# Small TensorE products in another order: array tiles alternate, first summands of all sums ahead of the second ones

## The chip, the cores and the metric

The kernel runs on one core of one Trainium2 chip. The metric is the device time of one execution in microseconds, the median of several runs. One core has TensorE (matrix products; in the profile PE for the matmuls and PEld for the weight loads), VectorE (DVE), ScalarE (ACT), GpSimd (POOL) and SyncE (SP, which here only issues DMAs).

## The reference

One layer of a decoder: a head group with an RWKV-7 recurrence and a head group with a gated linear recurrence side by side, then a mixture of experts, for a prompt of 1024 tokens and 8 decode tokens. The change touches the RWKV-7 recurrence alone. Per head (8 heads of 64 channels) the reference computes, token by token:

```python
def _wkv7_scan(r, decay, k, v, a_vec, b_vec, s0):
    def step(s, inp):
        r_t, w_t, k_t, v_t, a_t, b_t = inp
        sa = jnp.einsum('bhij,bhj->bhi', s, a_t)
        s = s * w_t[:, :, None, :] + sa[..., None] * b_t[:, :, None, :] + v_t[..., None] * k_t[:, :, None, :]
        return s, jnp.einsum('bhij,bhj->bhi', s, r_t)
```

Around it stand the input projection, small low-rank gates, a normalisation per head, the output projection (`w_out`) and the experts.

## The kernel before, in words

All data are f32. The kernel does not go token by token. It takes the heads in pairs (`j`, 4 pairs: 2 x 64 channels fill 128 partitions) and the tokens in chunks of 64, solves the dependence inside a chunk by products with a triangular inverse, and carries the state from chunk to chunk.

For each pair `j` TensorE first projects the tokens (`project_tile`, L791), and then makes two **passes** (`hf` = 0, 1), one for each half of the 1024 tokens. A pass has two groups (`g` = 0, 1) of 256 tokens. Each group has its own buffers (`grp[g]`) and its own four of the eight banks of PSUM (`q.bank(0)` to `q.bank(3)`). In all there are 4 pairs x 2 passes x 2 groups = 16 groups. Inside a group `hh` is one of the two heads of the pair (partitions 0 to 63 or 64 to 127, the slice `r`), `a` one of two blocks of 128 tokens (two chunks each), and `c` the first or second chunk of a block (partitions 0 to 63 or 64 to 127 where tokens are on partitions).

The order of TensorE in a pass is written out by hand:

- grams (L944) and transposes (L968), whose results VectorE masks and ScalarE copies;
- stages akv, u, w, z, each for group 0 and then for group 1, through the helper `stage` (L929); these products use all 128 rows and columns of the array, and between two stages VectorE or ScalarE brings the result to SBUF;
- stage `rt_mm` for group 0, then for group 1, in three parts: part 1 (L929), 4 products into `bank(0)` with 128 rows and 64 columns of the array, the columns chosen by the head; part 2 (L929), 8 products of 64 rows and 64 columns into `bank(2 + c)`; part 3 (L1004, L1005), 8 sums of two products each, 64 rows and 64 columns, into other columns of `bank(2 + c)`. The rows of parts 2 and 3 go by `c`, the columns by `hh`, so that `(c, hh)` is one of four quadrants of the array. The last product increments `rt_mm`;
- `y_products(0)`: 4 sums of two products (L1010, L1012), 128 rows, the columns by the head;
- `state_step(0, 0)`: the new state (L1030, two products) and its share of y (L1034, two products);
- `y_products(1)`, `state_step(0, 1)` to `(0, 3)`, `state_step(1, 0)` to `(1, 3)`, with grams or chunks of the next pair's projection (`keys_chunk`) between them, and then the normalisation of y.

On VectorE `transitions(g)` waits for `rt_mm`, adds into `rh` (L1830), makes four transition matrices `tt` (L1833) and copies part 3's sums into `into` (L1835). `next_state(g, n)` (L1841) waits for the state step's product and adds `into`. VectorE's order is transitions(0), next_state(0, 0), transitions(1), next_state(0, 1) and so on. `state_step(g, 0)` waits for `tt` and `rh`, every other state step for the sum before it.

The order of `heads()` before was `for hh in range(2): for a in range(2)`. It sets the order in grams, akv, u, w, z, the three parts of `rt_mm`, and y.

Behind the fourth pair come the output projection (L1104), the routing, and 20 steps of the experts. SP issues the loads of the projection weights by counts of TensorE's products (`win_mm`), the first loads of the experts' weights after the output projection (`wo_mm`), and later ones by TensorE's counts in the experts.

Of the kernel before, what the change touches and what calls it, by code (L numbers as in the profile page):

```python
# [21 lines left out]
HEAD = 64  # L22
# [40 lines left out]
def build(nc, x_all, c_t, shift_t, wkv0, conv0, lru0, state_conv, w_ada, b_ada, w_in, w_lo, prm, mu_lo,  # L63
# [9 lines left out]
    with ExitStack() as ctx:  # L73
# [356 lines left out]
        V, A, T, G = nc.vector, nc.scalar, nc.tensor, nc.gpsimd  # L430
# [313 lines left out]
        def _(pe):  # L744
# [72 lines left out]
            for c in range(3):  # L817
                c0, w = COLS[c]
                pe.wait_ge(win_out, c + 1)
                for m in range(2):  # L820
                    for g in range(4):
                        k = 2 * g + m
                        mm = T.matmul(ps[32 * g:32 * g + 32, c, 0:w], wlo[:, k, 128:160], hT[:, k, c0:c0 + w],
                                      start=(m == 0), stop=(m == 1))
# [3 lines left out]
            for c in range(3):  # L828
# [3 lines left out]
                         stop=True).then_inc(ad_mm, 1)  # L832
            pe.wait_ge(ld_const, 16 * 9)
            pe.wait_ge(ld_samp, 16 * 4)
            for j in range(NJ):
# [8 lines left out]
                def one_head(t):  # L844
                    return t.rearrange("p (h c) -> p h c", c=HEAD)[:, :, 0]
# [68 lines left out]
                for hf in range(2):  # L914
# [2 lines left out]
                    AR0, AR1, bb, k2, Bh, Kh, eP, rkp = kept[hf]  # L917
                    AR = ARs[hf]
                    def heads():
                        for hh in range(2):  # L920
                            for a in range(2):
                                yield hh, a, slice(HEAD * hh, HEAD * hh + HEAD)

                    def stage(g, name, waits, products, last=True):
                        gi = 2 * it + g
                        for w in waits:
                            pe.wait_ge(HV[w], gi + 1)
                        for out, lhs, rhs in products:
                            mm = T.matmul(out, lhs, rhs, start=True, stop=True)  # L929
                        if last:  # L930
                            mm.then_inc(HV[name], 1)
# [8 lines left out]
                    def grams(m, n, g, src):  # L940

                        q = grp[g]
                        for hh, a, r in heads():
                            mm = T.matmul(q.bank(2 * n + hh)[:, 256 * a:256 * a + 256], src[r, toks(g, a)],  # L944
                                          ARs[m][r, :, toks(g, a)], start=True, stop=True)
                        mm.then_inc(HV[("gram_b", "gram_k")[n]], 1)
# [27 lines left out]
                    for g in range(2):  # L974
                        q = grp[g]
                        stage(g, "akv_mm", ("tok_out",),
                              [(q.bank(3)[:, P * a + HEAD * hh:P * a + HEAD * hh + HEAD], q.ak[:, hh, a, 0, :],
                                q.vtok[:, a, HEAD * hh:HEAD * hh + HEAD]) for hh, a, r in heads()])
                    pe.wait_ge(p_in, 80 * (j + 1))
                    for g in range(2):  # L980
                        q = grp[g]
                        stage(g, "u_mm", ("dt_out", "akv_out"),
                              [(zunit(g, 0)[:, :, a, hh], pinv(hf, g)[:, hh, a], q.z[:, :, a, hh]) for hh, a, r in heads()])
                    for g in range(2):
                        q = grp[g]
                        stage(g, "w_mm", ("u_out",),
                              [(zunit(g, 1)[:, :, a, hh], q.dtg[:, hh, a, 0, :], q.u[:, :, a, hh]) for hh, a, r in heads()])
                    for g in range(2):
                        q = grp[g]
# [3 lines left out]
                    for g in range(2):  # L993
                        q = grp[g]
                        stage(g, "rt_mm", ("z_out",),
                              [(q.bank(0)[r, P * a:P * a + P], q.z[:, 0, a, hh, :], q.dtg[:, hh, a, 1, :])
                               for hh, a, r in heads()] +
                              [(q.bank(2 + c)[r, HEAD * a:HEAD * a + HEAD], q.zt[HEAD * c:HEAD * c + HEAD, 0, a, r],
                                q.btok[HEAD * c:HEAD * c + HEAD, a, r]) for c in range(2) for hh, a, r in heads()], False)
                        for c in range(2):  # L1000
                            t_ = slice(HEAD * c, HEAD * c + HEAD)
                            for hh, a, r in heads():
                                out = q.bank(2 + c)[r, 128 + HEAD * a:128 + HEAD * a + HEAD]
                                T.matmul(out, q.btok[t_, a, r], q.zt[t_, 1, a, r], start=True, stop=False)  # L1004
                                mm = T.matmul(out, q.ktok[t_, a, r], q.vtok[t_, a, r], start=False, stop=True)  # L1005
                        mm.then_inc(HV["rt_mm"], 1)
                    def y_products(g):
                        q = grp[g]
                        for hh, a, r in heads():
                            T.matmul(q.bank(1)[r, P * a:P * a + P], q.z[:, 1, a, hh, :], q.dtg[:, hh, a, 1, :],  # L1010
                                     start=(a == 0), stop=False, skip_group_check=True)
                            T.matmul(q.bank(1)[r, P * a:P * a + P], q.vtok[:, a, r], q.ak[:, hh, a, 1, :],  # L1012
                                     start=False, stop=False, skip_group_check=True)

                    def state_step(g, n):
# [20 lines left out]
                        if n == 3:  # L1036
                            mm.then_inc(HV["y_mm"], 1)

                    y_products(0)
                    state_step(0, 0)  # L1040
                    y_products(1)
                    for n in range(1, 4):
                        state_step(0, n)
# [21 lines left out]
                    for n in range(4):  # L1065
                        mm = T.matmul(bank[5][:, 2 * n:2 * n + 2], tmp[:, P * n:P * n + P], one_head(blk_mean),
                                      start=True, stop=True)
# [6 lines left out]
                    for n in range(4):  # L1074
                        for hh in range(2):
                            mm = T.matmul(bank[7][HEAD * hh:HEAD * hh + HEAD, P * n:P * n + P],
                                          gnorm[:, 2 * n + hh:2 * n + hh + 1].to_broadcast([P, HEAD]), ident,
                                          start=True, stop=True)
# [5 lines left out]
            for b_, lhs, rhs in ((4, w_up, pwd), (5, a_up, pad_), (6, g_up, pgd)):  # L1084
                for j in range(NJ):
                    mm = T.matmul(bank[b_][:, DEC * j:DEC * j + DEC], lhs[:, P * j:P * j + P],
                                  rhs[:, PAD + SEQ:PAD + NTOK], start=True, stop=True)
# [3 lines left out]
                     stop=True).then_inc(SAMP["s_norm"][0], 1)  # L1091
            for a, w_ in ((0, rg), (1, ig)):
                for j in range(NJ):
                    mm = T.matmul(bank[7][:, SN * a + DEC * j:SN * a + DEC * j + DEC], w_[:, j, :], s_xc[:, j, :],
                                  start=True, stop=True)
# [47 lines left out]
            def route_h2(i):  # L1143
# [3 lines left out]
                for k in range(KC):  # L1147
# [8 lines left out]
                     stop=True).then_inc(SAMP["s_bonmm"][0], 1)  # L1156
            pe.wait_ge(*SAMP["s_vec"])
            pe.wait_ge(*SAMP["s_lexp"])
            for q in range(6):
                mm = T.transpose(bank[6 + q // 4][0:SN, P * (q % 4):P * (q % 4) + P], s_vflat[:, SN * q:SN * q + SN], ident)  # L1160
# [20 lines left out]
            for i in (7, 8):  # L1181
# [7 lines left out]
                     stop=True).then_inc(rank_mm, 1)  # L1189
            pe.wait_ge(tile_col, 1)  # L1190
            T.matmul(bank[3][0:1, 0:NTILE], tcol[0:NTILE], ident[0:NTILE, 0:NTILE], start=True,
                     stop=True).then_inc(tile_row, 1)
            for n in range(18):
                if n % 6 == 0:
                    pe.wait_ge(hot_ready, n // 6 + 1)
                c = n % NCT
                mm = T.matmul(bank[2][COLT * c:COLT * c + COLT, 0:P], wt[:, n // 9, n % 9, :], uu[:, n, :],
                              start=(n < NCT), stop=(n >= 18 - NCT))
# [61 lines left out]
            for i, t in enumerate(LAST):  # L1260
# [5 lines left out]
                for n in range(2):  # L1266
                    for a in range(2):
                        mm = T.matmul(ps[0:rt, 2 * (i % 4) + n, :], wdiag[t][0:rt, P * a:P * a + rt],  # L1268
                                      yg[t][0:rt, a, 512 * n:512 * n + 512], start=(a == 0), stop=(a == 1))
# [1005 lines left out]
```

## Time and profile before

| | before |
|---|---|
| median of 3 runs | 1248.86 us (1244.17 to 1253.95) |
| the profiled execution | 1248.42 us, its span 1246.4 us |
| TensorE matmuls busy | 1089.4 us, 87% |
| VectorE busy | 639.0 us, 51% |
| ScalarE busy | 306.0 us, 25% |
| granted TensorE clock, mean | 0.933 |

The span is the time from the first to the last instruction of the program on the core. Busy times of different engines overlap. The granted clock is the share of TensorE's full clock that the chip gave it: 1.00 is 2.4 GHz, 0.5 is 1.2 GHz. Starts of matmuls are recorded, their ends are modelled; one product of f32 leaves two matmul records and two weight loads.

### The profile page before, as it was taken

The page shows a single profiled execution, that of the slowest core. Times are in us where ns is not written, and L with a number is a line of the kernel's source. Part 1 is how long each engine was busy: PE and PEld are TensorE (multiplying, and loading weights), DVE is VectorE, ACT ScalarE, POOL GpSimd, SP SyncE. Part 2 cuts the span into 40 slices and gives each one's busy share as a digit, 9 for nine tenths or more (in the row PEclk, how much of TensorE's full clock was granted, in tenths as well). Part 3 has the DMA queues.
Part 4 walks back from the last instruction along what each step waited for, and adds up shares of the span by engine and source line. Part 5 has one row for each costly group of instructions (what it writes and reads, how often), then busy time and mean ns, then how long its engine had stood idle before and what let it go on. Part 6 is the DMA issues. An engine that isn't in the chain of part 4 may idle for free.

```text
span 1246.4 us, 18940 instructions
## 1 busy us (share of the span) xinstructions
PE 1089.4 (87%) x7309; PEld 635.8 (51%) x7309; DVE 639.0 (51%) x1298; ACT 306.0 (25%) x576; POOL 87.6 (7%) x142
## 2 busy tenths in 40 slices
PE   5899997999979999899997799997388989899692
PEld 3445566766667666676666654554232333233131
DVE  7326684268942689425894349988501111111158
ACT  2324241142411424114141240111011111111246
POOL 4210100000000010000100010000000000000050
PEclk9999999999989999889999889998588999899976
DMA  9965310011100111000140061224867795866472
GB/s 354 295 218 187 103 34 2 1 34 52 35 1 1 34 52 34 1 1 23 30 154 1 1 236 51 74 90 148 324 219 286 257 351 198 294 219 211 147 288 118
DMA packets 56625, 160.78 MB, mean 129 GB/s; under 512 B 23512, under 2 KB 23720, under 8 KB 50776
## 3 DMA queue, kind: packets, MB, share of 16 engines
q1 hardware_dynamic: 46376, 126.40, 29.8%
q0 software_dynamic: 6560, 22.07, 5.1%
q10 hardware_dynamic: 3600, 11.11, 2.3%
q8 instruction: 57, 0.93, 0.3%
q14 instruction: 32, 0.26, 0.1%
HBM read 341.48 MB, written 22.59 MB: 292 GB/s over the span
## 4 chain that ended last, share of the span: by engine, by line
PE 54%; DVE 23%; SPq 8%; DMA 8%; issue 5%; ACT 1%; POOL 0%; DVEq 0%; POOLq 0%; ACTq 0%
PE ps L791 14%; PE ps L1104 7%; PE ps L1214 5%; PE ps L929 5%; PE ps L1229 4%; DVE arena L1753 3%; DVE arena L1755 3%; DMA arena<-in_w_ada 3%; SPq L534 3%; DMA arena<-in_w_dn 3%; PE ps L1030 2%; SPq L565 1%; SPq L561 1%; DVE arena L1768 1%; PE ps L751 1%
## 5 line engine op out<-in xcount | busy, mean ns | idle before, releaser
L791 PE MATMUL ps<-arena 128*128 128x348 f32 (+1 forms) x1008 | 306.7, 460 | 2.5 <-DVE arena L1620 2.5
L791 PEld LDWEIGHTS ps<-arena 128*128 128x128 f32 x1008 | 189.4, 191 | 114.6 <-issue 19.3
L1214 PE MATMUL ps<-arena 128*32 128x512 f32 x1280 | 149.2, 615 | 9.7 <-DMA arena<-in_w_gu 8.4
L2150 DVE COPY arena<-ps 128x1024 f32<-128x1024 f32 x20 | 24.5, 1226 | 177.1 <-PE ps L1229 177.1
L1104 PE MATMUL ps<-arena 128*128 128x512 f32 x256 | 114.1, 601 | 0.0
L1214 PEld LDWEIGHTS ps<-arena 128*32 128x32 f32 x1280 | 43.6, 113 | 110.8 <-issue 101.4
L1229 PE MATMUL ps<-arena 128*32 128x512 f32 x640 | 78.9, 637 | 12.6 <-DMA arena<-in_w_dn 12.2
L929 PE MATMUL ps<-arena 128*128 128x128 f32 (+3 forms) x896 | 86.2, 278 | 3.8 <-DVE arena L1825 2.8
L929 PEld LDWEIGHTS ps<-arena 128*128 128x128 f32 (+2 forms) x896 | 79.4, 179 | 10.6 <-DVE arena L1825 3.6
L1104 PEld LDWEIGHTS ps<-arena 128*128 128x128 f32 x256 | 48.3, 193 | 56.8 <-issue 56.7
L1319 ACT ACTIVATE arena<-ps 128x348 f32<-128x348 f32 (+1 forms) x54 | 24.8, 460 | 205.4 <-PE ps L791 198.5
L1229 PEld LDWEIGHTS ps<-arena 128*32 128x32 f32 x640 | 21.1, 115 | 55.7 <-issue 55.0
L1268 PE MATMUL ps<-arena 128*128 128x512 f32 (+1 forms) x72 | 37.5, 687 | 8.7 <-DMA arena<-slot_scr,arena 8.7
L944 PE MATMUL ps<-arena 64*128 64x256 f32 x256 | 35.5, 411 | 9.5 <-DVE arena L1875 6.7
L1753 DVE TENSOR_TENSOR arena<-arena 64x30 f32<-64x30 f32 (+14 forms) x120 | 39.8, 332 | 6.6 <-POOL arena L688 2.6
L2144 DVE TENSOR_TENSOR arena<-arena,ps 128x256 f32<-128x256 f32 x20 | 8.5, 423 | 67.0 <-ACT arena L1503 67.0
L1841 DVE TENSOR_TENSOR arena<-ps,arena 128x64 f32<-128x64 f32 x64 | 14.3, 224 | 54.8 <-PE ps L1030 54.8
L1755 DVE TENSOR_TENSOR arena<-arena 64x30 f32<-64x30 f32 (+14 forms) x120 | 38.8, 323 | 4.1
L1503 ACT ACTIVATE arena<-ps 128x256 f32<-128x256 f32 x20 | 7.7, 385 | 133.7 <-PE ps L1214 133.7
L725 POOL DMA_INDIRECT arena<-h_scr,arena x20 | 18.9, 945 | 274.9 <-PE ps L1206 210.2
L682 POOL MEMSET arena<- 128x2048 f32 x4 | 7.2, 1806 | 440.1 <-DVE arena L1717 440.1
L1402 ACT ACTIVATE arena<-ps 128x512 f32<-128x512 f32 (+1 forms) x48 | 25.3, 526 | 43.0 <-PE ps L929 42.8
(421 smaller groups left out, 1515.0 us busy)
## 6 DMA issues: line engine op xcount, KB each, us to landing
arena<-in_w_gu SPq DMA_DIRECT2D x336, 512.0 KB
arena<-in_w_dn SPq DMA_DIRECT2D x84, 1024.0 KB
arena<-in_w_ada SPq DMA_DIRECT2D x24, 1024.0 KB, 6.1
arena<-in_w_in SPq DMA_DIRECT2D x20, 512.0 KB, 3.8
slot_scr<-arena ACTq DMA_DIRECT2D x20, 512.0 KB, 4.1
arena<-in_x_all SPq DMA_DIRECT2D x16, 512.0 KB, 4.9
arena<-in_w_out SPq DMA_DIRECT2D x8, 512.0 KB, 7.4
h_scr<-arena SPq DMA_DIRECT2D x8, 512.0 KB, 2.6
```

The costliest lines, as they stand in the source:

```text
L534: sp.dma_start(exgu_f[c][:, cols], src, cond=ch[c]).then_inc(ld_gu[h], 16)
L791: mm = T.matmul(ps[0:rows, c, 0:w], lhs(k), hT[:, k, c0:c0 + w], start=(k == 0), stop=(k == KC - 1))
L929: mm = T.matmul(out, lhs, rhs, start=True, stop=True)
L944: mm = T.matmul(q.bank(2 * n + hh)[:, 256 * a:256 * a + 256], src[r, toks(g, a)], ARs[m][r, :, toks(g, a)], start=True, stop=True)
L1030: mm = T.matmul(out[r], q.tt[r, n, :], S[r, n % 2, :], start=True, stop=True)
L1104: mm = T.matmul(ps[0:rt, 2 * (i % 2) + n, :], yT[:, k, r0:r0 + rt], wout[:, k, 512 * n:512 * n + 512], start=(k == 0), stop=(k == KC - 1))
L1214: mm = T.matmul(ps[r_, 2 + b, :], xgt[b][:, k, r_], exgu[c][:, k, :], start=(k == 0), stop=(k == KC - 1))
L1229: mm = T.matmul(ps[r_, 6 + n, :], hidt[b][:, q, r_], exdn[c][:, q, 512 * n:512 * n + 512], start=(q == 0), stop=(q == 1))
L1268: mm = T.matmul(ps[0:rt, 2 * (i % 4) + n, :], wdiag[t][0:rt, P * a:P * a + rt], yg[t][0:rt, a, 512 * n:512 * n + 512], start=(a == 0), sto ...
L1402: A.activation(dst, src, ACT.Copy).then_inc(HV[name], 1)
L1753: link(TT(prod, m[:, 0:k, k:k + 1].to_broadcast([64, k, w]), m[:, k:k + 1, k + 1:32].to_broadcast([64, k, w]), ALU.mult))
L1755: last = TT(m[:, 0:k, k + 1:32], m[:, 0:k, k + 1:32], prod, ALU.add)
```

## The change

The two loops of `heads()` change places, part 2 has the chunk inside, part 3 goes through all four quadrants with the first summand of a block's sums and then with the second, and the y products do all first summands before the second ones. The products, their operands, outputs and waits are the same.

```diff
                     def heads():
-                        for hh in range(2):
-                            for a in range(2):
+                        for a in range(2):
+                            for hh in range(2):
                                 yield hh, a, slice(HEAD * hh, HEAD * hh + HEAD)
...
-                                q.btok[HEAD * c:HEAD * c + HEAD, a, r]) for c in range(2) for hh, a, r in heads()], False)
-                        for c in range(2):
-                            t_ = slice(HEAD * c, HEAD * c + HEAD)
-                            for hh, a, r in heads():
-                                out = q.bank(2 + c)[r, 128 + HEAD * a:128 + HEAD * a + HEAD]
-                                T.matmul(out, q.btok[t_, a, r], q.zt[t_, 1, a, r], start=True, stop=False)
-                                mm = T.matmul(out, q.ktok[t_, a, r], q.vtok[t_, a, r], start=False, stop=True)
+                                q.btok[HEAD * c:HEAD * c + HEAD, a, r]) for hh, a, r in heads() for c in range(2)], False)
+                        for a in range(2):
+                            for last, left, right in ((False, q.btok, q.zt[:, 1]), (True, q.ktok, q.vtok)):
+                                for hh in range(2):
+                                    r = slice(HEAD * hh, HEAD * hh + HEAD)
+                                    for c in range(2):
+                                        t_ = slice(HEAD * c, HEAD * c + HEAD)
+                                        mm = T.matmul(q.bank(2 + c)[r, 128 + HEAD * a:128 + HEAD * a + HEAD],
+                                                      left[t_, a, r], right[t_, a, r], start=not last, stop=last,
+                                                      skip_group_check=True)
                         mm.then_inc(HV["rt_mm"], 1)
                     def y_products(g):
                         q = grp[g]
                         for hh, a, r in heads():
                             T.matmul(q.bank(1)[r, P * a:P * a + P], q.z[:, 1, a, hh, :], q.dtg[:, hh, a, 1, :],
                                      start=(a == 0), stop=False, skip_group_check=True)
+                        for hh, a, r in heads():
                             T.matmul(q.bank(1)[r, P * a:P * a + P], q.vtok[:, a, r], q.ak[:, hh, a, 1, :],
                                      start=False, stop=False, skip_group_check=True)
```

## Rows read from the trace of the kernel before

**Rows 1.** The page: TensorE's busy time (share) and records; the chain by engine.
```profile
PE 1089.4 (87%) x7309; PEld 635.8 (51%) x7309; DVE 639.0 (51%) x1298; ACT 306.0 (25%) x576; POOL 87.6 (7%) x142
...
PE 54%; DVE 23%; SPq 8%; DMA 8%; issue 5%; ACT 1%; POOL 0%; DVEq 0%; POOLq 0%; ACTq 0%
```
**Rows 2.** Table of stretches, TensorE alone: rt of group 1, y of group 0.
```profile
core 0: us, PE busy (x), PEclk, DMA share, GB/s
...
344.86:347.16 2.30, 2.30 (x58) 1.00 0.00 0
347.16:348.67 1.51, 1.51 (x18) 1.00 0.05 11
```
**Rows 3.** Timeline (start, us, engine, line, count), TensorE: rt of group 1, y.
```profile
344.86 0.42 PEld L929 LDWEIGHTS ps<-arena 128*64 128x64 f32 x8
...
345.46 0.34 PEld L929 LDWEIGHTS ps<-arena 64*64 64x64 f32 x16 [0.17 <-issue]
...
345.74 0.28 PE L1004 MATMUL ps<-arena 64*64 64x64 f32 x2
...
345.86 0.28 PE L1005 MATMUL ps<-arena 64*64 64x64 f32 x2
...
345.97 0.33 PE L1004 MATMUL ps<-arena 64*64 64x64 f32 x4
...
346.84 0.28 PE L1004 MATMUL ps<-arena 64*64 64x64 f32 x2
...
347.16 0.43 PE L1010 MATMUL ps<-arena 128*64 128x128 f32 x2
...
347.43 0.38 PE L1012 MATMUL ps<-arena 128*64 128x128 f32 x2
...
347.65 0.44 PE L1010 MATMUL ps<-arena 128*64 128x128 f32 x4
...
348.14 0.38 PE L1010 MATMUL ps<-arena 128*64 128x128 f32 x2
...
348.67 0.33 PE L1030 MATMUL ps<-arena 64*64 64x64 f32 x4
```
**Rows 4.** The same timeline: VectorE's work, and the third state step on TensorE.
```profile
344.97 0.42 DVE L1830 TENSOR_TENSOR arena<-arena,ps 128x256 f32<-128x256 f32 x1 [3.84 <-PE ps L1005]
345.31 0.85 DVE L1833 SCALAR_TENSOR_TENSOR arena<-arena,ps 128x64 f32<-128x64 f32 x4
...
349.12 0.23 DVE L1841 TENSOR_TENSOR arena<-ps,arena 128x64 f32<-128x64 f32 x1 [2.63 <-PE ps L1030]
...
350.36 0.41 DVE L1835 COPY arena<-ps 128x256 f32<-128x256 f32 x1
...
351.01 0.22 DVE L1841 TENSOR_TENSOR arena<-ps,arena 128x64 f32<-128x64 f32 x1 [0.24 <-PE ps L1030]
...
351.29 0.33 PE L1030 MATMUL ps<-arena 64*64 64x64 f32 x4 [0.28 <-DVE arena L1841]
```
**Rows 5.** Timelines: products that alternate tiles, and the grams.
```profile
351.45 0.28 PE L1034 MATMUL ps<-arena 64*64 64x64 f32 x4
...
272.22 1.97 PE L872 MATMUL ps<-arena 128*64 128x128 f32 x32
...
326.69 3.80 PE L944 MATMUL ps<-arena 64*128 64x256 f32 x32 [0.69 <-ACT arena L1324]
```
**Rows 6.** Stretches from rt to rt, pairs 1 to 3: us, five engines, clock, DMA.
```profile
342.57:382.33 39.76, 33.09 (x350) 27.14 (x349) 14.47 (x35) 7.12 (x16) 0.00 (x0) 0.87 0.00 1
498.68:539.64 40.96, 34.85 (x350) 29.09 (x349) 14.47 (x35) 7.12 (x16) 0.00 (x0) 0.83 0.00 1
655.98:693.42 37.44, 30.66 (x349) 24.78 (x348) 14.47 (x35) 7.01 (x16) 0.00 (x0) 0.95 0.01 1
```
**Rows 7.** Groups by line and shape, all passes: records, busy us, mean ns.
```profile
L1004 PE MATMUL ps<-arena 64*64 64x64 f32 x256 | 22.0, 227 | 0.0
...
L1010 PE MATMUL ps<-arena 128*64 128x128 f32 x128 | 20.1, 285 | 0.0
```

## The prediction

> **What bounds the kernel now.** I read the page first: TensorE is busy 87% of the span and carries 54% of the chain that ended last, VectorE 23% [rows 1]. So an order on TensorE is worth something only in a stretch where that chain runs through TensorE without a break. The next view is a table of stretches inside one pass (group 1 of the first pass of pair 1): the stage `rt_mm` (2.30 us) and the y products (1.51 us) are filled by TensorE completely, at a granted clock of 1.00, the 2.4 GHz level [rows 2]. What is saved there moves everything behind it, until some other engine is late.
>
> The timeline of the same stretch tells how the array is used [rows 3]. A product leaves two matmul records: L1004 has 256 records for 16 groups of 8 products [rows 7]. The stage has three parts. Part 1, four products into the two column halves of bank 0, runs from 344.86 to 345.46, 0.60 us. Part 2, eight products in the four quadrants, from 345.46 to 345.74, 0.28 us: its 16 weight loads all lie within 0.34 us, so the four quadrants run side by side already, although the program gives each quadrant two products in a row. Part 3, sixteen products (L1004, L1005), from 345.74 to 347.16, 1.42 us. Here each quadrant gets four products in a row, and the rows show a staircase: x2, x2 alone, then three steps of x4, x4, then x2, x2 alone. Eight pairs of products take five steps, where two quadrants at most run together. The y products show it with halves: x2, x2, then x4, x4, then x2, x2: three steps of 0.49, 0.49 and 0.53 us.
>
> My reading of both: matmuls start in program order, and a tile of the array takes four records ahead. Four in a row for one tile leave the next tile free to start at once (parts 1 and 2); eight in a row hold it up until the fifth has started (part 3 and y).
>
> **The change part by part.** No instruction is added or removed, no DMA and no wait; every increment stays on the last product of its group. Only TensorE's order moves.
>
> (a) `heads()` now has the pair outside and the head inside. In akv, u, w and z every product fills all 128 rows and columns, so there is no other tile: nothing. In the grams a row half gets two products in a row, four records, within the reach above: 32 records of 256 columns stand in 3.80 us [rows 5], 0.11 us each, as long as a 128-column record alone in its half takes (0.109 us, below), so the halves overlap already: nothing. Parts 1 and 2: also nothing. A first start some 0.01 us sooner is the most I can see there, and I take 0.
>
> (b) Part 3, quadrants inside, summands outside. One quadrant alone does a pair (four records) in 345.97 - 345.74 = 0.23 us, 0.058 us a record. In the new order each quadrant still has eight records, but all four run together: 8 x 0.058 = 0.46 us. Behind the last record the next stage takes 0.09 us (the last lone pair starts at 346.84 and L1010 at 347.16, 0.32 less the 0.23 of its own records), and the four quadrants start one after another, three times about 0.014 us (16 loads of part 2, the last starting about 0.21 us after the first). Together 0.60 us instead of 1.42: **0.82 us a group**. Part 2 gives the same: 0.28 us for four rounds, 0.23 for four more, 0.09 behind.
>
> (c) The y products, first summands ahead. In one half a record takes 0.109 us (347.43 to 347.65 for two) and entering the form costs 0.05 (0.49 for the first four). Eight records in each half, side by side: 0.05 + 8 x 0.109 + about 0.11 behind and between = 1.03 us instead of 1.51: **0.48 us a group**. Part 1 again agrees: 0.60 us with four records in each half, plus 4 x 0.109.
>
> That alternating products overlap at all is shown in the trace: L872 alternates the column halves at every product, and 32 records of 128 columns stand in 1.97 us [rows 5], 0.06 us each against 0.109 alone. L1030 alternates quadrants at every product, and its four records are through in 0.16 us, 351.29 to 351.45 [rows 4, 5], where one quadrant after the other would need 0.23.
> The Trainium skill, page "TensorE: Matmul & The Clock Gate", Part 3 (The mechanism), speaks against (c): a weight load overlaps running matmuls only where the row group differs, and the column halves of y share all rows. L872 above disagrees with it. By that rule (c) would give nothing and (b) only the two row halves; what this makes of the sum is among the rivals.
>
> (d) What of it reaches the end. On TensorE the order in a pass is rt of group 0, rt of group 1, y of group 0, the first state step, y of group 1, the second state step. The first state step comes 0.82 + 0.82 + 0.48 = 2.12 us sooner. Its other wait, VectorE's transitions of group 0 (344.97 to about 346.2 [rows 4]), starts 0.82 sooner as well and is still done before. Then VectorE is late next: behind the first state sum (349.12) it does the transitions of group 1, whose last copy ends at 350.36 + 0.41 = 350.77, and the second sum starts at 351.01 after an idle of 0.24 us [rows 4]. All of this moves by 2.12; the 0.48 of group 1's y can only eat that idle time, less some 0.04 us for the hand-over: 0.20. From there a state step waits for VectorE's sum and the sum for the state step (L1030 at 351.29 idled 0.28 for it), so the rest of the pass keeps its length. **2.12 + 0.20 = 2.32 us a pass.** There are four pairs with two passes each, 16 groups [rows 7]: 8 x 2.32 = 18.6 us.
>
> Behind a pass nothing is tied to the clock on the wall: the next pair's projections wait for TensorE and ScalarE, the queue on SP loads the next weights by TensorE's counts, and the experts' first loads wait for the output projection (`wo_mm`). So the gain should stay. The profiled execution took 1248.42 us (0.44 under the median of 1248.86): 1248.42 - 18.6 = **1230 us**. With no VectorE limit it would be 8 x 2.60 = 20.8, 1228 us.
>
> **The clock as spread.** Between the `rt` stages of the two passes of a pair the granted clock falls to half for a while, and that stretch takes 40.96 us at a mean of 0.83 and 37.44 us at 0.95 [rows 6]; pair 1 takes 39.76 at 0.87, and pair 0 the same within 0.02 us. Which stretches are slow will be dealt anew when all moves by 2 us. Four like the best would be 149.8 instead of 157.9 us (-8), four like the worst 163.8 (+6). I take about 4 us either way.
>
> **The rivals.**
> 1. *Issue is the limit.* Parts 2 and 3 are 24 products in 1.70 us, 0.071 us each; if the sequencer gives no more, part 3 keeps its length but for a head start during part 1 (0.60 us for four products, 0.32 us to spare). Gain per rt 0 to 0.31, per pass 0.68 to 1.3, in all 5 to 10 us: 1238 to 1243. Against it: part 2 starts its loads at 0.014 us each, and the y staircase has the same shape at 0.12 us a product, where issue can't be the limit.
> The same page of the Trainium skill ("Wait — 56ns, not 53.3ns?") gives about 62 ns a matmul where the sequencer's microcode decodes; an estimate by it is 1234 us, and no run here shows which decoder is on.
> 2. *Column halves don't overlap.* Then y gives nothing and part 3 runs two-fold: 16 x 0.058 + 0.13 = 1.06, 0.36 a group, 0.72 a pass, 5.8 us: 1243. L872 and part 1 speak against it.
> 3. *The clock gives it back.* TensorE's work in a pass becomes shorter while its waits stay. From 37.44 to 39.74 us the mean falls from 0.95 to 0.87, about 6.8 us more at half clock for 2.3 us. To eat 18.6 us, each pair needs 14 us more of half clock: 1240 to 1249. The stretch in rows 2 ran at 1.00 throughout and gets denser, so I see no reason.
> 4. *Slower: tiles take turns.* If neighbours in other tiles ran one after the other, part 3 would need 16 x 0.117 + 0.13 = 2.0 us (+0.58) and y 8 x 0.219 + 0.16 = 1.91 (+0.40): 1.96 a pass, 16 us, 1264. It decides once fewer than about 1.4 tiles run together. L1030 and L872 speak against it.
>
> **How the numbers follow.** The forecast 0.66 (1222 to 1236: the sum, its bounds and the clock), rival 1 0.14, rival 2 0.04, rival 3 0.08, rival 4 0.03, and 0.05 for a clock even better than 1222. The range reaches from 1222 to 1240: the forecast and most of rival 1. One per cent, about what a measurement of this kernel can tell from no change, is 1236.4 on the faster side: faster 0.72 (the forecast, the 0.05 and a little of rival 1), no change 0.25 (the rest of rivals 1 to 3), slower 0.03.
>
> **What would show it.** Right: in the timeline, part 3 without staircase and about 0.6 us from its first record to the next stage, y about 1.03; rt stage about 1.48 us a group; VectorE's second sum with no idle before it; the stretch from the first `rt` record of group 0 to the third state step shorter by 2.3 us in all eight passes. Wrong: part 3 at 0.07 us a product (rival 1), y at 1.5 us (rival 2), a lower clock in `rt` (rival 3). The prediction fails most easily if something behind the passes that I take for tied to TensorE keeps its own time.

## The result

| | before | after |
|---|---|---|
| median | 1249.8 us (10 runs) | 1236.55 us (10 runs) |
| ratio to before, 95% interval | | 0.9914, 0.9887 to 0.9941 |
| the profiled execution, its span | 1248.42, 1246.4 us | 1234.13, 1232.2 us |
| TensorE matmuls busy | 1089.4 us | 1069.7 us |
| mean granted clock of the profiled execution | 0.933 | 0.927 |

The kernel became faster by about one per cent. The ratio gives a gain of 7 to 14 us, the two medians 13 us; 18.6 us were forecast. In two later comparisons, on two chips, the ratio was 0.9874 (0.9831 to 0.9918, e5_after) and 0.9899 (0.9865 to 0.9933, e12_after). The time lies in the stated range of 1222 to 1240 us, but above the 1222 to 1236 us that belonged to the forecast itself; the last 4 us of the range were there for rival 1.

In the code after the change the lines lie a little lower: part 3 is L1006, the y products L1013 and L1016, the state step L1034 and L1038, the state sum L1845. The timeline of the same stretch as [rows 3, 4], the first pass of pair 1 in the profile of after:

```profile
338.73 0.42 PEld L929 LDWEIGHTS ps<-arena 128*64 128x64 f32 x8
...
339.32 0.32 PEld L929 LDWEIGHTS ps<-arena 64*64 64x64 f32 x16 [0.17 <-issue]
...
339.60 0.65 PE L1006 MATMUL ps<-arena 64*64 64x64 f32 x32
...
340.18 0.66 PE L1013 MATMUL ps<-arena 128*64 128x128 f32 x8
...
341.20 0.33 PE L1034 MATMUL ps<-arena 64*64 64x64 f32 x4
...
341.65 0.22 DVE L1845 TENSOR_TENSOR arena<-ps,arena 128x64 f32<-128x64 f32 x1 [1.25 <-PE ps L1034]
...
342.89 0.42 DVE L1839 COPY arena<-ps 128x256 f32<-128x256 f32 x1
343.34 0.23 DVE L1845 TENSOR_TENSOR arena<-ps,arena 128x64 f32<-128x64 f32 x1
343.62 0.33 PE L1034 MATMUL ps<-arena 64*64 64x64 f32 x4 [0.57 <-DVE arena L1845]
```

The staircase is gone. Part 3 runs from 339.60 to 340.18, 0.58 us instead of 1.42, and y from 340.18 to 341.20, 1.02 us instead of 1.51. The second state sum (343.34) has no idle before it any more, and TensorE's wait for it grew from 0.28 us [rows 4] to 0.57. From the first `rt` record (337.29) to the third state step (343.62) are 6.33 us; before, 342.57 to 351.29, 8.72. That is 2.39 us, where 2.32 were forecast.

The table of stretches is the best ruler for the whole kernel, since one stretch is free of the clock: from the `rt` stage of a pair's second pass to that of the next pair's first pass. The columns are start:end, us, TensorE busy, granted clock, DMA share, GB/s. First before:

```profile
226.23:342.57 116.34, 112.41 (x690) 1.00 0.12 33
382.33:498.68 116.35, 112.40 (x689) 1.00 0.12 33
539.64:655.98 116.34, 112.40 (x690) 1.00 0.18 56
```

and after (here with all five engines):

```profile
223.32:337.29 113.97, 109.66 (x690) 75.07 (x689) 78.24 (x174) 36.42 (x64) 3.88 (x4) 1.00 0.13 33
374.61:488.60 113.99, 109.66 (x689) 75.07 (x688) 78.26 (x174) 36.42 (x64) 3.88 (x4) 1.00 0.12 33
527.17:641.12 113.95, 109.65 (x689) 75.07 (x688) 78.19 (x174) 36.41 (x64) 4.99 (x6) 1.00 0.18 57
```

Three times 2.36 to 2.39 us less, at a clock of 1.00 on both sides; 8 x 2.37 = 19.0 us. The stretches between the two passes of a pair, which answer to [rows 6], do not all show it:

```profile
337.29:374.61 37.32, 30.38 (x349) 24.71 (x349) 14.49 (x35) 7.12 (x16) 0.00 (x0) 0.86 0.00 1
...
641.12:678.44 37.32, 30.39 (x349) 24.71 (x348) 14.49 (x35) 7.12 (x16) 0.00 (x0) 0.86 0.01 1
```

For pair 1 it is 2.44 us (39.76 before), for pair 3 only 0.12 (37.44 before, at a clock of 0.95). And the last stretch, from the last pass's `rt` to the first product of the output projection, became longer, first before, then after:

```profile
693.42:724.36 30.94, 24.37 (x280) 0.77 0.24 84
```
```profile
678.44:709.79 31.35, 24.55 (x279) 0.65 0.23 82
```

So the profile itself points to the clock: 0.65 instead of 0.77 in a stretch whose work is 2.4 us shorter. Each run comes with its span and mean clock. As the clock has two levels, 1.00 and 0.5, the time at the half one is 2 x (1 - clock) x span; all times at half clock below are worked out in this way or, for single falls, read from the clock records of a trace. The experiments below ask two things: which edit saves the work, and whether it is the clock that takes part of it back.

### The profile page after: what moved, and what is told of

The parts are those of the page before. It is cut to its first block, busy times and chain, and to the rows that moved or that the text cites. A ratio compares the mean times of both kernels' runs of the same rounds, so it can differ in the third digit from the quotient of the medians.

```text
span 1232.2 us, 18940 instructions
## 1 busy us (share of the span) xinstructions
PE 1069.7 (87%) x7309; PEld 616.7 (50%) x7309; DVE 639.2 (52%) x1298; ACT 306.2 (25%) x576; POOL 87.6 (7%) x142
## 4 chain that ended last, share of the span: by engine, by line
PE 53%; DVE 25%; DMA 9%; SPq 7%; issue 5%; ACT 1%; POOL 0%; DVEq 0%; POOLq 0%; ACTq 0%
PE ps L791 14%; PE ps L1108 7%; PE ps L1218 6%; PE ps L929 5%; PE ps L1233 4%; DMA arena<-in_w_dn 3%; DVE arena L1757 3%; DVE arena L1759 3%; DMA arena<-in_w_ada 3%; SPq L534 2%; PE ps L1034 1%; DVE arena L1772 1%; SPq L561 1%; SPq L565 1%; PE ps L751 1%
## 5 line engine op out<-in xcount | busy, mean ns | idle before, releaser
L929 PEld LDWEIGHTS ps<-arena 128*128 128x128 f32 (+2 forms) x896 | 82.1, 184 | 10.1 <-DVE arena L1829 3.6
L1845 DVE TENSOR_TENSOR arena<-ps,arena 128x64 f32<-128x64 f32 x64 | 14.3, 224 | 42.4 <-PE ps L1034 42.1
```

## The experiments

All of them ran beside the kernel before. "Next-pair stretch" is the one of 116.34 us above, read in each profile.

**e1_part3: part 3 alone.** Against the kernel before:

```diff
-                        for c in range(2):
-                            t_ = slice(HEAD * c, HEAD * c + HEAD)
...
-                                T.matmul(out, q.btok[t_, a, r], q.zt[t_, 1, a, r], start=True, stop=False)
-                                mm = T.matmul(out, q.ktok[t_, a, r], q.vtok[t_, a, r], start=False, stop=True)
+                        for a in range(2):
+                            for last, left, right in ((False, q.btok, q.zt[:, 1]), (True, q.ktok, q.vtok)):
+                                for hh in range(2):
...
+                                    for c in range(2):
...
+                                                      left[t_, a, r], right[t_, a, r], start=not last, stop=last,
```

> Part 3 of the rt stage in the new order, all else as before. If a tile takes four records ahead (theory 1): part 3 without staircase, the rt stage 1.45 us a group instead of 2.30, y unchanged at 1.51. The first state step then comes 2 x 0.85 = 1.70 us sooner and nothing else does: the stretch from the second pass of a pair to the next pair, 116.34 us before, takes 114.64, and all eight passes give 13.6 us less what the clock takes. If the accumulating neighbours were what held part 3 up, the same; if the new order of heads() were needed for it (rival), part 3 stays above 1 us.

Measured: `rt` 1.47 us a group, and y 1.51 with its staircase. The next-pair stretch:

```profile
226.26:340.97 114.71, 110.77 (x690) 1.00 0.13 33
```

1.63 us less than before; 1.70 were expected. The median of 4 runs is 1234.05 us, ratio 0.9887 (0.9841 to 0.9933), with as much half clock as the kernel before beside it (165 us a run in both). Part 3 alone carries most of the work saved, and it needs no new `heads()`. Its ratio is that of the whole change (0.9874 to 0.9914): what the other half, the new y order, saves besides can't be seen in the time.

**e2_y: the y products alone.**

```diff
-                        for hh, a, r in heads():
+                        order = [(hh, a, slice(HEAD * hh, HEAD * hh + HEAD)) for a in range(2) for hh in range(2)]
+                        for hh, a, r in order:
                             T.matmul(q.bank(1)[r, P * a:P * a + P], q.z[:, 1, a, hh, :], q.dtg[:, hh, a, 1, :],
                                      start=(a == 0), stop=False, skip_group_check=True)
+                        for hh, a, r in order:
                             T.matmul(q.bank(1)[r, P * a:P * a + P], q.vtok[:, a, r], q.ak[:, hh, a, 1, :],
```

> The y products in the new order, all else as before. Theory 1: y takes 1.02 us instead of 1.51; the first state step comes 0.49 us sooner, and of the second 0.49 VectorE's transitions let 0.20 through: the stretch to the next pair 116.34 - 0.69 = 115.65 us, 5.5 us in all. If VectorE did not limit (rival): 116.34 - 0.98 = 115.36.

```profile
230.67:346.33 115.66, 111.43 (x689) 1.00 0.12 33
186.85:230.67 43.82, 38.19 (x349) 0.73 0.01 1
```

The next-pair stretch falls by 0.68 us, as expected to 0.01: of the second y only what VectorE's idle time allows. But the time did not fall: 1250.29 us median of 10, ratio 1.0023 (0.9997 to 1.0049). Mean clock 0.926 instead of 0.934; 185 us at half clock instead of 165. The second row shows one place: between the first two passes the clock was 0.73 on average, and the stretch took 43.82 us instead of 39.74. The four stretches of this kind hold 58 us of half clock in e2's profile and 38 in that of before.

**e3_heads: `heads()` and part 2 alone,** part 3 and y in the old order.

> Only heads() and part 2 of rt in the new order; part 3 and y in the old one. Theory 1: at most two products per tile in a row before, so nothing changes: part 1 and 2 at 0.60 and 0.28 us, the stretch to the next pair 116.34 us, within 0.05. Rival (alternating at every product is worth something for the grams and parts 1 and 2): the stretch is shorter by 0.1 us or more.

```profile
228.12:344.46 116.34, 112.33 (x689) 1.00 0.12 33
```

116.34 us, nothing, and 1248.01 us, ratio 1.0001 (0.9972 to 1.0029). In the grams and in parts 1 and 2, two products per tile in a row were no hindrance.

**e4_adjacent and e6_adjacent: as after, but both summands of a sum side by side again,** so that each tile gets two products in a row:

```diff
-                            for last, left, right in ((False, q.btok, q.zt[:, 1]), (True, q.ktok, q.vtok)):
-                                for hh in range(2):
...
-                                    for c in range(2):
...
+                            for hh in range(2):
...
+                                for c in range(2):
...
+                                    T.matmul(out, q.btok[t_, a, r], q.zt[t_, 1, a, r], start=True, stop=False,
...
+                                    mm = T.matmul(out, q.ktok[t_, a, r], q.vtok[t_, a, r], start=False, stop=True,
...
-                        for hh, a, r in heads():
                             T.matmul(q.bank(1)[r, P * a:P * a + P], q.vtok[:, a, r], q.ak[:, hh, a, 1, :],
```

> As after, but the two summands of a sum stand side by side again, in part 3 and in y: each tile gets two products (four records) in a row, and then the next tile. Theory 1 (four records are taken ahead): as fast as after, rt 1.45 and y 1.02 us, the stretch to the next pair 113.97 us; first summands ahead of second ones is worth nothing by itself. Rival (a second summand right behind the first waits for it, and that held the others up): the staircase comes back in part, rt above 1.7 us, y above 1.2, the stretch above 114.7 us.

```profile
225.74:339.96 114.22, 109.96 (x689) 1.00 0.12 33
```

114.22 us: neither 113.97 nor above 114.7. Per group `rt` takes 1.55 us and y 1.07, so two products per tile in a row cost about 0.1 and 0.05 us here; the staircase does not come back. "First summands ahead" is thus worth 0.25 of the 2.37 us a pass, the alternation of tiles the rest. Whether the 0.25 us comes from a second summand right behind its first, as the rival has it, or from two products in a row whatever they are, e4 does not tell; part 2, which has no sums, took 0.28 us in either order. e4's 1231.94 us (4 runs) with a clock of 0.931 led to the idea that the alternation at every y product lowers the clock. e6 tested this beside e5_after (the changed kernel again) on one chip.

> The changed kernel, unchanged, beside the next three and the kernel before. Over the runs so far the kernel before spends 165 us of a run at the half clock (mean clock 0.934), the changed one 184 us (0.925), e2_y 185 us, e1_part3, e3_heads and e4_adjacent 165 to 169; a microsecond at half clock costs 0.31 to 0.35 us. Theory 2: the new y order brings more half clock, about 20 us a run, which costs 6 to 7 us of the 18.9 us of work saved: clock 0.925 again and 1236 us. Rival: the lower clock belongs to the chip or the hour of the first runs: clock 0.933 and 1230 us.

> e4_adjacent once more, now beside the changed kernel on one chip. Theory 2 (the alternation of halves at every y product lowers the clock, pairs of products do not): clock 0.931, 1232 us, some 4 us under e5_after. Rival (e4's four runs were lucky, both have the same short y): clock and time as e5_after within 1.5 us, or slower by the 0.25 us a pass that the work is longer (2 us).

e5_after: 1233.42 us, ratio 0.9874 (0.9831 to 0.9918), mean clock 0.929, between what was expected (0.925, 1236 us) and its rival (0.933, 1230 us). e6_adjacent: 1234.73 us, 0.9876 (0.9827 to 0.9925), 0.930. The two are the same within these intervals, and theory 2 falls in this form: the alternation at every y product is not what moves the clock.

**e8_three: six records per quadrant in a row.** Part 3 of after with three products of each quadrant, then the fourth of each:

```diff
+                        for n0, n1 in ((0, 3), (3, 4)):
+                            for hh in range(2):
...
+                                for c in range(2):
...
+                                    for n in range(n0, n1):
+                                        a, last = n // 2, n % 2 == 1
+                                        left, right = (q.ktok, q.vtok) if last else (q.btok, q.zt[:, 1])
...
```

> The changed kernel, but part 3 gives each quadrant three products (six records) in a row and then the fourth. If a tile takes four records ahead: the next quadrant starts when the third record of the one before starts, 0.117 us later, three times: part 3 is longer by 0.35 us a group (rt 1.80), 0.70 a pass, and the stretch to the next pair takes 113.97 + 0.70 = 114.67 us. If more are taken ahead (rival): 113.97; if fewer, above 115.

The rule holds, and its price was higher. In the records a quadrant's first three start at 339.720, 339.779 and 339.837, and the next quadrant's first at 339.843, 6 ns behind the third of six. The fourth quadrant starts 0.46 us behind the first (340.184), since from the second on a quadrant's first record needs about 0.107 us (339.843 to 339.949) and not 0.058; the last round pays it again. The next-pair stretch:

```profile
223.93:338.85 114.92, 110.64 (x689) 1.00 0.12 33
```

0.95 us over after, where 0.70 was expected. Its time, of a single run, is 1242.93 us.

**e7_fill: TensorE's waits filled.** The changed kernel with 38 products that compute nothing needed, and a wait for `dt_out` ahead of some of them:

```diff
+                    def filler(n):
+                        for _ in range(n):
+                            T.matmul(bank[0][:, 0:384], ident, rg[:, 0:3, :], start=True, stop=True, skip_group_check=True)
...
                         pe.wait_ge(HV["y_roots"], 2 * it)
                         grams(1, 0, 1, bb)
+                        filler(3)
                         pe.wait_ge(HV["half_done"], it)
                     grams(hf, 1, 1, k2)
+                    if hf:
+                        filler(3)
                     for g in range(hf, 2):
                         turn(hf, g)
...
+                    if hf == 0:
+                        pe.wait_ge(HV["dt_out"], 2 * it + 3)
+                    if hf == 0 or j == NJ - 1:
+                        filler(2)
                     pe.wait_ge(HV["y_roots"], 2 * it + 1)
...
+            for _ in range(4):
+                T.matmul(bank[0][:, 0:384], ident, rg[:, 0:3, :], start=True, stop=True, skip_group_check=True)
             pe.wait_ge(HV["half_done"], 2 * NJ)
```

> The changed kernel with products that compute nothing needed, put where TensorE waits: in the first pass of each pair 2 (before the row of squares), 3 (before the mask of y is done) and 3 (before the last turn), in the last pass 2 and 4. Each is 384 columns, about 0.67 us at full clock, into a bank that is free. If idle TensorE in these places is what lowers the clock (theory 2): the stretch between the two passes of a pair loses its half clock (37.3 us before filling, 34 to 35 with a clock above 0.97), the clock rises to 0.945 or more and the time falls by 8 to 12 us under e5_after. Rival (the clock falls for another reason, or the fillers stand in the way): the stretch stays at 37 us or grows by up to 5 us.

1220.51 us, ratio 0.9773 (0.9730 to 0.9816), mean clock 0.946. Where the clock stayed up, the stretch between the two passes takes 34.49 us:

```profile
338.02:372.51 34.49, 31.67 (x366) 1.00 0.00 1
```

against 37.32 at 0.86 in after. This holds for two of the four pairs; in the other two the clock fell to half 8.4 us behind `rt`, for 10.2 and 6.8 us, and the stretch took 38.03 and 36.52 us. More work on TensorE made the kernel 13 us faster than e5_after beside it. The timeline of after shows the waits that were filled:

```profile
353.60 1.05 PE L1070 MATMUL ps<-arena 128*128 128x2 f32 x8 [1.44 <-ACT arena L1430]
...
359.57 1.54 PE L944 MATMUL ps<-arena 64*128 64x256 f32 x8 [1.90 <-DVE arena L1879]
362.43 1.97 PE L968 MATMUL ps<-arena 128*128 128x128 f32 x8 [1.32 <-DVE arena L1780]
```

Behind the second of these waits eight gram records take 1.54 instead of 1.13 us, and behind the third the transposes 1.97 instead of 1.07: these are products at half clock.

**e9_before_fill, e10_fill, e12_after: the change with the clock out of the way.** The filler of e7 in the kernel before, in the changed one again, and the changed kernel without it, on one chip.

> The kernel before, with the same products in TensorE's waits as e7_fill (they compute nothing needed). Theory 3: the change saves 18.6 us of work whatever the clock does, and the clock takes a part back because more of a run is at half clock (175 to 184 us against 165). With the waits filled in both kernels the clock has little to take: this kernel about 1237 us (before less some 12 us), e10_fill 18 to 19 us under it. Rival (the change saves less work than the stretches say, or something behind the passes keeps its own time): the two filled kernels differ by 13 us or less, as the unfilled ones do.

> The changed kernel with the filled waits once more, beside e9_before_fill, on one chip. 1220 us and a clock of 0.946 as in e7_fill, 18 to 19 us under e9_before_fill by theory 3, 13 or less by its rival.

> The changed kernel on the chip of the three above. Theory 3: more half clock than the kernel before beside it (0.925 to 0.929 against 0.933), 1234 to 1237 us, and at equal half clock, taken at 0.33 us a microsecond, 18 to 19 us less than before.

| | median us | ratio to before | mean clock | us at half clock |
|---|---|---|---|---|
| before (11 runs) | 1252.24 | 1 | 0.931 | 173 |
| e12_after (6) | 1237.97 | 0.9899 (0.9865 to 0.9933) | 0.924 | 188 |
| e9_before_fill (6) | 1234.5 | 0.9863 (0.9834 to 0.9892) | 0.954 | 113 |
| e10_fill (6) | 1219.05 | 0.9732 (0.9700 to 0.9764) | 0.949 | 124 |

The change is worth 14.3 us without fillers here and 15.5 us with them: neither 18 to 19 nor 13. Half clock is not equal in the filled kernels either, 124 against 113 us. The profiles say where. First e9, then e10: between the passes, to the next pair, and the last stretch.

```profile
186.63:223.54 36.91, 34.35 (x365) 1.00 0.01 2
223.54:339.88 116.34, 112.41 (x690) 1.00 0.12 33
683.30:711.09 27.79, 25.29 (x292) 0.94 0.18 65
```
```profile
188.81:223.29 34.48, 31.66 (x365) 1.00 0.01 2
223.29:338.93 115.64, 111.35 (x689) 0.99 0.12 33
671.97:698.24 26.27, 23.64 (x292) 0.89 0.18 60
```

Between the passes both have the full clock, and the change shows its 2.43 us. In the next stretch, and in one more like it, e10 has lost all but 0.70 of 2.37: the clock fell to half 8.6 us behind the `rt` stage, in the run of state steps, for 3.4 us.

**e11_chain: one product more in the state steps.**

```diff
                     for n in range(1, 4):
                         state_step(0, n)
+                        if n == 1:
+                            T.matmul(bank[2][:, 0:256], ident, rg[:, 0:2, :], start=True, stop=True, skip_group_check=True)
```

> e10_fill with one more product of 256 columns that computes nothing needed, between the second and the third state step of each pass, where TensorE now waits 0.57 us for VectorE. In the profiles of the changed kernel the clock fell 9.4 us behind the last pass's rt stage, in the run of state steps, for 27 us; in those of the kernel before 16.9 us behind it, for 17. If the longer wait in the state steps is what lets the clock fall there (theory 4), the fall goes: clock above 0.950 and 3 us or more under e10_fill. Rival (it is the state steps themselves, which one product doesn't change): the clock as in e10_fill and the time the same within 1.5 us, or up to 2 us longer where the product does not fit into the wait.

```profile
186.73:221.21 34.48, 32.22 (x368) 1.00 0.01 2
221.21:335.18 113.97, 110.22 (x691) 1.00 0.12 33
666.54:691.42 24.88, 22.66 (x293) 0.95 0.18 63
```

Its profile has no falls in the state steps, and all stretches are at their best: 24.88 us for the last is 2.91 less than e9. Over the runs the clock is 0.952, as expected above 0.950, where e10 has 0.949. The time is 1217.94 us, only 1.1 under e10 and not 3, which is what the rival expected; the two ratios are both 0.9732 (e11 0.9703 to 0.9762, e10 0.9700 to 0.9764).

e9 and e11 give a second ruler for the work: from the first `rt` record to the first product of the output projection, all eight passes ran almost wholly at full clock in both (3.5 and 2.4 us at half). First e9, then e11:

```profile
186.63:711.09 524.46, 499.94 (x3812) 1.00 0.10 31
```
```profile
186.73:691.42 504.69, 482.24 (x3827) 1.00 0.11 31
```

That is 19.8 us less, beside 8 x 2.37 = 19.0. Behind the passes e11's profile is longer: the experts took 265.5 us from their first to their last gate-and-up product, in e10's 260.1 and in e9's 258.9. In e11 TensorE waited 24.1 us in all for the DMAs of their weights (e10 23.2, e9 20.9), and the stretch had 26 us of half clock (16 and 19). Whether the change has a part in this, or whether it varies so from run to run, is not shown.

## Why the prediction was right and where it failed

**The look-ahead: right.** A tile of the array takes work ahead and the next tile starts only when enough of it is under way: e3 (two in a row cost nothing in the parts that it changed; the sums of e4 paid 0.25 us a pass), e8 (six records in a row: the next tile starts at the third) and after (one in a row: no staircase). In e8 as in [rows 3] three records of a tile may wait behind the one that has just started.

**(a) nothing, (b) 0.82, (c) 0.48 us a group: right.** e3 gave 0.00 us a pass, `rt` came down by 0.85, y by 0.49. e1 alone gave 1.63 us a pass, e2 alone 0.68, together 2.31; measured for both 2.37.

**(d) VectorE limits the second y: right.** In e2, y saves 2 x 0.49 us of TensorE's time and the pass gets 0.68. The idle time moved from VectorE to TensorE: the 0.24 us before the sum [rows 4] are gone, and TensorE's 0.28 us before the third state step became 0.57.

**Behind the passes nothing keeps its own time: right as far as the profiles tell.** From the first product of the output projection to the end the profile of before has 1246.4 - 724.36 = 522.0 us and that of after 1232.2 - 709.79 = 522.4. One profile each is a coarse ruler here: over all fourteen this stretch took 518.4 to 524.7 us.

**The clock: wrong, and this is the step that failed.** The prediction took it as a spread of 4 us either way, and left rival 3 a chance of 0.08, because the `rt` stage runs at 1.00 and gets denser. It does, and still does at 1.00. What was not asked is what becomes of the stretch behind it. That the time still lies in the stated range is in part luck: 18.6 us less than the median of 1249.8 would be 1231.2, and the 4 us between 1236 and 1240 were added for rival 1, which falls. Over all runs of the two kernels whose clock is known (of the ten of before in the first comparison it is not):

| | mean span us | us at half clock |
|---|---|---|
| before (41 runs, three comparisons) | 1247.9 | 167.5 |
| after (22 runs, three comparisons) | 1234.8 | 183.0 |

Within the runs of one kernel a microsecond more at half clock goes with 0.31 us more of span (one common slope for the kernels with several runs, e11 not among them; 0.28 in the kernel before alone, 0.36 in the changed one; the prediction had 2.3 / 6.8 = 0.34 from [rows 6]). So an estimate is that 15.5 us x 0.31 = 4.8 us of the gain went to the clock, and 13.1 + 4.8 = 17.9 us is the work, beside 18.6 forecast and 8 x 2.37 = 19.0 from the stretches. Side by side on one chip the changed kernel had 9 us more at half clock (e5, 176 against 167) and 15 us more (e12, 188 against 173), which is 2.7 and 4.7 us. e2 shows it at its sharpest: 8 x 0.68 = 5.4 us saved, 18 us more at half clock than all runs of before, no gain left.

Where the additional half clock lies, the profiles tell in part. With the y of before (before, e1, e3, e9: 32 passes) the clock never fell 8 to 12 us behind the `rt` stage. With the short y (after, e2, e4 to e8, e10, e12: 72 passes) it did so 13 times, 7 of them in the last pass, where no projection of a next pair follows. There the fall came 9.4 us behind `rt` in all three profiles of the changed kernel and lasted 27.3 us; in before, 16.9 us behind and 17.1 us. After's last pass in steps of 3 us:

```profile
681.44:684.44 3.00, 2.77 (x48) 1.00 0.02 5
684.44:687.44 3.00, 1.79 (x32) 1.00 0.00 0
687.44:690.44 3.00, 2.70 (x18) 0.57 0.00 0
690.44:693.44 3.00, 2.20 (x3) 0.50 0.00 0
```

and before's in its state steps and behind them:

```profile
702.42:705.42 3.00, 1.97 (x38) 1.00 0.00 0
705.42:708.42 3.00, 2.37 (x12) 1.00 0.00 0
708.42:711.42 3.00, 1.34 (x10) 0.81 0.00 0
```

In after TensorE went through its state steps, busy 1.79 of 3.00 us and waiting for VectorE in between, and then the clock fell; in before it was still at 1.00 in the 3 us behind the state steps. The two products behind the state steps paid for it: 2.07 and 1.91 us in after at half clock, 1.12 and 1.02 in before, both on the chain.

That the falls 8 to 12 us behind `rt` come with the short y is what these profiles show. That the wait before the third state step, which grew from 0.28 to 0.57 us, is their cause is plausible, but not shown. For it speaks e11, which puts a product into this wait and had none of these falls in its eight passes, where e10 had three. But with 13 falls in 72 passes, eight passes without one would come by chance in about one case of five. Against it as the whole cause speaks e2: it has the same wait of 0.57 us and only one such fall, in its first pass; in its last pass the clock fell 16.3 us behind `rt` and for 17.1 us, as in before. Most of e2's additional half clock lies between the passes.

Between the passes the cause is open. Before, e1 and e3 had 3 to 17 us of half clock in such a stretch, never the same in all four pairs. The three profiles of the changed kernel agree in pairs 1 to 3 (10.2, 13.6 and 10.2 us) and differ only in pair 0 (10.2 to 17.0), so their half clock is not a matter of chance alone.

**The rivals.**

1. Issue limits: falls. Parts 2 and 3 are 24 products in 0.86 us, 0.036 us each.
The Trainium skill's figure of about 62 ns a matmul ("TensorE: Matmul & The Clock Gate", section "Wait — 56ns, not 53.3ns?") does not hold in this program; its case is microcode decoding.
2. Column halves don't overlap: falls, y took 1.02 us.
The rule of the Trainium skill, same page, Part 3 (The mechanism), on weight loads in one row group, which would have brought it, is not what y shows here.
3. The clock gives it back: true for about 3 to 5 of 18 us, at about the price per microsecond that it named.
4. Tiles take turns: falls, part 3 took 0.58 us.

## What to carry to other kernels

Where small products use a half or a quadrant of TensorE's array, let neighbours in the program use different tiles: here one product each in turn took 0.58 us where four in a row per tile took 1.42; two in a row took 0.1 us more than one. Then look at what TensorE does behind the shortened stretch: here its wait grew there and more time at half clock came with the change, and by estimate 3 to 5 us of 18 went with it. Waits of TensorE may be worth filling even with products that nobody needs: 13 to 19 us in this kernel (e7 to e5, e9 to before, e10 to e12), and 1219 us together with the change.

## What the runs showed of the hardware

- The first record of a tile that takes over costs about 0.05 us more than the next (0.107 against 0.058 in the quadrants of e8), so handing over between tiles is not free; in after, where all four enter together, it is paid once (339.320 to 339.427, at the start of part 2).
- In after four quadrants start 6 to 7 ns apart in each round (338.156, .163, .169, .176, and the next round at .214). Before, with two products per tile in a row, part 2's were 13 ns apart.
- The clock costs the kernel before more than the prediction's whole gain: some 167 us of it are spent at 1.2 GHz, and at 0.31 us each an estimate is 52 us. Filling waits of 1.3 to 3 us with 38 products in all took some 60 us of it away (e9 113 us against 173 in before beside it, e10 124 against 188 in e12).
